# Rope and mixed key/value blocks from PSUM, gates copied raw, and the conv norm in another bank

## The chip, the core and the metric

The kernel runs on one core of a Trainium2 chip. The metric is the device time of one execution in microseconds. TensorE (PE) multiplies, VectorE (DVE), ScalarE (ACT) and GpSimd (POOL) do the rest on tiles of 128 partitions, and SyncE (SP) issues most DMAs. Each engine runs its own list of instructions in order; semaphores tie them together. Only TensorE, VectorE and ScalarE reach PSUM, which has 8 banks of 512 float32 per partition.

## The reference

Two blocks that share no data are computed in one program. The first is a hybrid state-space block (an SSD mixer and an S5 mixer, then an MLP). The second is a two-layer block on 512 latent tokens and 256 context tokens. The change is mostly in the second one's mixer. Cut to what matters:

```
p = h @ w_in                       # conv a|g, q, k, v, gates
q, k = rope_2d(q), rope_2d(k)
u = a * sigmoid(g); u = dwconv1d(u, 31 taps); u = silu(layernorm(u, ln_g, ln_b))
y_conv = u @ w_conv_out
y_attn = neighbourhood_attention(q, k, v, k_ctx, v_ctx, rpb) @ w_na_out
g_conv, g_attn = split(sigmoid(gates))
x = x + g1 * ((g_conv * y_conv + g_attn * y_attn) @ w_out)
```

Rope is `x * cos + rot(x) * sin`. Queries lie on a grid of 8 rows and 64 columns; each tile of 16 columns looks at a window of keys, and two of the six stored blocks of 128 keys are mixed from halves of two others.

## The kernel before

**Units.** All weights come as units of 128 output rows by 1024 inputs (512 KB). `U` counts them; unit g uses slot g % 4 (R = 4) of the weight buffers and of the PSUM accumulators. For a unit SyncE loads `wraw`, ScalarE copies it to `whi` (`split_hi`, line 257), GpSimd subtracts to `wlo` (`split_lo`, line 265), and TensorE makes three products for each of 8 input tiles (`pe_unit`, line 304, and `pe_quad` for four units together, line 338). `unit_done[s]` tells that a unit is finished, `acc_free[s]` that its accumulator has been read. A next load into a slot waits for the split or, where units are used whole (pass c0, `p.one`), for `unit_done`.

**Passes.** The second block has the passes c0 (context, layer 0, 256 columns, whole units), l0 (latent, layer 0, 512 columns), c1 (context of layer 1, keys and values only: `kv_pe`, `kv_act`, `kv_dve`) and l1. c0, l0 and l1 run `mix_*` and then `merge_*`, with units `p.U` to `p.U + 35` in the mixer: 8 for the conv branch, 12 for q, k, v of four head pairs, 16 gates. The merge has `M = p.U + 36` to `M + 7`.

**Attention.** 16 tiles in l0 and l1 (4 head pairs by 4 column tiles), 8 in c0. In each tile TensorE does the scores (`scores_pe`), transposes the probabilities of the tile before (`turn_pe`), makes the values of the one before that (`values_pe`), and one unit in between (`pe_filler`, lines 1945 to 1949; two in c0), whose result `pe_post` turns or transposes into bank 3. VectorE adds the bias and takes the maximum (`top_dve`), does a step of rope or of the values (`post_dve`), the reciprocal (`scale_dve`), and one or two rounds of conv taps (`conv_taps`, line 2240). ScalarE reads out the units (`evac_act`), exponentiates (`exps_act`, line 2106) and scales (`scale_act`). GpSimd does the conv taps of two more tiles and the `wlo` splits. The order is written out by hand in `mix_pe`, `mix_act`, `mix_dve` and `mix_pool`. `pe_post` of a step waits for the VectorE step before (`x_v`). The remaining conv taps of VectorE come after the last tile.

**Merge.** `merge_pe` multiplies the attention half of units M to M+3 (input tiles 4 to 7, banks 4 to 7), and in between the conv layernorm: a mean, a variance and a row of factors, all three in bank `p.U % R`, which is the bank of unit M's conv half. The conv halves of units M+1 to M+3 then go first, and unit M's follow. `merge_dve` multiplies by the gates `gt`.

**Other places.** `s5_pe` ends the S5 mixer with `ada_turn(7)`; ScalarE's `ada_cols(7)` and the last Gelu wait for it in order. `raw_pe` follows `ssd_pe`. `keep_busy(pe, bank, n)` is n products of 256 columns whose result nobody reads.

Of the kernel before, what the change touches and what calls it, by code (L numbers as in the profile page):

```python
# [120 lines left out]
def build(nc, A, out, ud, yd, pd):  # L121
# [1343 lines left out]
    def s5_pe(pe):  # L1465
# [8 lines left out]
        for i in range(NT):  # L1474
# [291 lines left out]
    rt = at("rt", [P, SEQ], O_HL + 12 * K)  # L1766
# [110 lines left out]
    def kv_act(act, p, then):  # L1877
# [3 lines left out]
        norm_root_act(act, n, then.T, "eps6")  # L1881
        for j in range(4):
            s, rnd = slot(p.U + j)
            act.wait_ge(unit_done[s], rnd + 2)
            act.activation(kctx[:, j], ps[:, s, 0:p.T], ACT.Copy).then_inc(acc_free[s], 1)
            split_hi(act, p.U + j + R)
# [183 lines left out]
    def evac_act(act, p, g):  # L2070
# [56 lines left out]
    def mix_act(act, p):  # L2127
# [40 lines left out]
        act.activation(lst[:, 0, 0:T // P], ps[:, p.U % R, 0:T // P], ACT.Sqrt, bias=col("eps6")).then_inc(p.c_a.sem, 1)  # L2168
# [9 lines left out]
    def post_dve(dve, p, i):  # L2178
# [3 lines left out]
        if k == 2:  # L2182
            v = ps[:, 3, 0:p.T].rearrange("p (b d) -> p b d", d=P)
            if p.lat:
                dve.tensor_copy(vT[:, 0:2], v[:, 0:2])
                dve.tensor_copy(vT[:, 4:6], v[:, 2:4])
                dve.drain()
                for m_, (lo, hi) in MIX.items():
                    dve.tensor_copy(vT[0:64, m_], vT[0:64, lo])
                    ins = dve.tensor_copy(vT[64:P, m_], vT[64:P, hi])  # L2190
            else:
                ins = dve.tensor_copy(vctx[:, :, h * P:(h + 1) * P], v)
        else:
# [49 lines left out]
    def mix_dve(dve, p):  # L2243
# [45 lines left out]
        for m in range(4):  # L2289
            dve.tensor_tensor(cn[:, m, 0:T], co[:, m, 0:T], ps[:, p.U % R, 0:T], ALU.subtract).then_inc(p.c_v.sem, 1)  # L2290
# [903 lines left out]
```

## Time and profile before

| | us |
|---|---|
| median of 3 runs | 2962.23 (2959.38 to 2964.63) |
| the profiled execution | 2951.68, span 2949.4 |
| TensorE busy | 2816.3 (95%) |
| VectorE busy | 1537.3 (52%) |
| GpSimd busy | 1274.6 (43%) |
| ScalarE busy | 1116.2 (38%) |
| mean granted TensorE clock | 0.981 of full |

Times in the trace count from the span's start. c0's mixer ends at about 1150 us and its merge at 1185. The attention of l0 runs from 1263 to 1456, its merge to 1546. c1 lies about 2143 to 2190, the attention of l1 from 2238 to 2430, its merge to 2520. Matmuls are pipelined and their ends are modelled, so a busy TensorE is not one at its peak; idle time in front of an instruction is named with what ended it. A granted clock of 1.00 is 2.4 GHz, of 0.50 1.2 GHz.

### The profile page before, as it was taken

The page shows a single profiled execution, that of the slowest core. Times are in us where ns is not written, and L with a number is a line of the kernel's source. Part 1 is how long each engine was busy: PE and PEld are TensorE (multiplying, and loading weights), DVE is VectorE, ACT ScalarE, POOL GpSimd, SP SyncE. Part 2 cuts the span into 40 slices and gives each one's busy share as a digit, 9 for nine tenths or more (in the row PEclk, how much of TensorE's full clock was granted, in tenths as well). Part 3 has the DMA queues.
Part 4 walks back from the last instruction along what each step waited for, and adds up shares of the span by engine and source line. Part 5 has one row for each costly group of instructions (what it writes and reads, how often), then busy time and mean ns, then how long its engine had stood idle before and what let it go on. Part 6 is the DMA issues. An engine that isn't in the chain of part 4 may idle for free.

```text
span 2949.4 us, 41217 instructions
## 1 busy us (share of the span) xinstructions
PE 2816.3 (95%) x15658; PEld 2297.0 (78%) x15658; DVE 1537.3 (52%) x1968; ACT 1116.2 (38%) x1666; POOL 1274.6 (43%) x696
## 2 busy tenths in 40 slices
PE   7999988999999999989999999999989999999998
PEld 6975734878888877867777888888877777788887
DVE  6865585353323255278775432423355867552525
ACT  4445223333323233236633422322343573342433
POOL 3444101435445173388842322222347784444443
PEclk9999998999999999999999999999999999999999
DMA  4235497323233233432222212122223222333332
GB/s 174 95 101 212 135 314 250 95 93 100 91 95 99 93 123 122 143 93 83 68 86 65 72 55 74 57 65 65 72 86 114 76 68 72 100 93 94 99 94 78
DMA packets 116008, 306.88 MB, mean 104 GB/s; under 512 B 36176, under 2 KB 44496, under 8 KB 115344
## 3 DMA queue, kind: packets, MB, share of 16 engines
q1 hardware_dynamic: 87584, 284.49, 30.5%
q10 hardware_dynamic: 27712, 18.50, 2.2%
q8 instruction: 100, 1.64, 0.2%
q0 software_dynamic: 560, 1.84, 0.2%
q14 instruction: 52, 0.43, 0.0%
HBM read 294.95 MB, written 7.45 MB: 103 GB/s over the span
## 4 chain that ended last, share of the span: by engine, by line
PE 77%; DVE 8%; DVEq 4%; ACT 3%; issue 2%; POOL 2%; DMA 2%; ACTq 1%; SPq 0%; POOLq 0%
PE ps L304 38%; PE ps L338 17%; PE ps L329 6%; PE ps L1941 3%; DVEq L2241 2%; POOL wlo L265 2%; DVE co L2240 2%; PE ps L2352 2%; PE ps L1945 1%; PE ps L1946 1%; PE ps L1949 1%; DMA mt<-ka 1%; PE ps L748 1%; DVE nacc L451 1%; PE ps L1999 1%
## 5 line engine op out<-in xcount | busy, mean ns | idle before, releaser
L265 POOL TENSOR_TENSOR wlo<-wraw,whi 128x1024 fp32r<-128x1024 f32 x373 | 923.1, 2484 | 1360.7 <-ACT whi L257 1359.3
L257 ACT ACTIVATE whi<-wraw 128x1024 fp32r<-128x1024 f32 x373 | 392.3, 1055 | 458.2 <-PE ps L304 170.5
L304 PE MATMUL ps<-xah,whi 128*128 128x512 f32 x992 | 387.9, 391 | 1.7 <-issue 1.7
L304 PE MATMUL ps<-xal,whi 128*128 128x512 f32 x992 | 387.4, 391 | 0.0
L304 PE MATMUL ps<-xah,wlo 128*128 128x512 f32 x992 | 280.1, 391 | 0.0
L2240 DVE SCALAR_TENSOR_TENSOR co<-ub,vec,co 128x512 f32<-128x512 f32 (+1 forms) x216 | 247.7, 1186 | 5.4 <-issue 0.4
L304 PEld LDWEIGHTS ps<-xah,whi 128*128 128x128 f32 x992 | 186.1, 188 | 42.8 <-issue 2.7
L304 PEld LDWEIGHTS ps<-xal,whi 128*128 128x128 f32 x992 | 186.1, 188 | 40.3
L304 PEld LDWEIGHTS ps<-xah,wlo 128*128 128x128 f32 x992 | 186.1, 188 | 40.2
L2339 POOL TENSOR_TENSOR co<-co,ct 128x512 f32<-128x512 f32 (+1 forms) x144 | 168.1, 1167 | 21.7 <-issue 1.8
L304 PE MATMUL ps<-hhi,whi 128*128 128x512 f32 x408 | 159.3, 390 | 1.1 <-ACT whi L257 1.1
L304 PE MATMUL ps<-hlo,whi 128*128 128x512 f32 x408 | 158.8, 389 | 0.0
L1109 DVE SCALAR_TENSOR_TENSOR res<-ps,mod,res 128x512 f32<-128x512 f32 (+1 forms) x64 | 47.7, 749 | 201.6 <-PE ps L329 110.0
L2687 DVE SCALAR_TENSOR_TENSOR f<-ps,vec,f 128x511 f32<-128x511 f32 x88 | 50.2, 612 | 196.6 <-ACT f L2648 196.6
L1945 PE MATMUL ps<-xah,whi 128*128 128x512 f32 x352 | 145.5, 413 | 4.2 <-DVE ub L2252 2.6
L2337 POOL TENSOR_TENSOR ct<-ub,vec 128x512 f32<-128x512 f32 (+1 forms) x144 | 136.5, 948 | 22.5 <-issue 12.4
L1946 PE MATMUL ps<-xal,whi 128*128 128x512 f32 x352 | 139.3, 396 | 0.0
L2645 ACT ACTIVATE f<-ps,vec 128x512 f32<-128x512 f32 x44 | 34.3, 780 | 186.9 <-PE ps L329 179.1
L1107 DVE TENSOR_TENSOR res<-res,ps 128x512 f32<-128x512 f32 x48 | 33.0, 688 | 132.2 <-PE ps L304 70.2
L304 PE MATMUL ps<-hhi,wlo 128*128 128x512 f32 x408 | 100.9, 389 | 0.0
L329 PE MATMUL ps<-xchi,whi 128*128 128x256 f32 x352 | 99.5, 283 | 0.0
L329 PE MATMUL ps<-xchi,wlo 128*128 128x256 f32 x352 | 99.3, 282 | 0.0
(419 smaller groups left out, 6065.1 us busy)
## 6 DMA issues: line engine op xcount, KB each, us to landing
wraw<-stream SPq DMA_DIRECT2D x425, 512.0 KB, 3.5
wada<-w_ada SPq DMA_DIRECT2D x56, 512.0 KB, 7.4
wraw<-w_ada SPq DMA_DIRECT2D x40, 512.0 KB, 3.9
biasb<-attn_bias ACTq DMA_DIRECT2D x32, 256.0 KB, 3.6
xin<-x0T SPq DMA_DIRECT2D x4, 528.0 KB, 6.7
s_u<-uk ACTq DMA_DIRECT2D x8, 264.0 KB, 2.5
res<-x0T ACTq DMA_DIRECT2D x1, 2048.0 KB, 9.5
outT<-res SPq DMA_DIRECT2D x4, 512.0 KB, 2.6
```

What stands on the lines that cost most here:

```text
L257: act.activation(whi[:, s], wraw[:, s], ACT.Copy).then_inc(hi_done[s], 1)
L265: pool.tensor_tensor(wlo[:, s], wraw[:, s], whi[:, s].bitcast(F32), ALU.subtract).then_inc(lo_done[s], 1)
L304: last = pe.matmul(ps[:, bank, 0:b - a], w[:, s, kt], x[:, kt, c0 + a:c0 + b], start=start, stop=stop)
L329: return pe.matmul(ps[:, R + s, 0:CTX], w[:, s, kt], part[:, kt], start=start, stop=stop)
L338: last = pe.matmul(ps[:, bank, 0:b - a], w[:, s, kt], x[:, kt, c0 + a:c0 + b], start=start, stop=stop)
L1941: last = pe.matmul(o, wraw[:, s, kt], x1[:, kt, 0:p.T], start=kt == 0, stop=kt == NT - 1)
L1945: pe.matmul(o, whi[:, s, kt], xah[:, kt, 0:p.T], start=kt == 0, stop=False)
L1946: pe.matmul(o, whi[:, s, kt], xal[:, kt, 0:p.T], start=False, stop=False)
L2240: dve.scalar_tensor_tensor(o, ub[:, m, k:k + p.T], colr(f"dw{p.l}", 1, k * 4 + m), o, ALU.mult, ALU.add)
L2241: dve.drain()
L2337: pool.tensor_tensor(ct[:, 0:T], ub[:, m, k:k + T], colr(f"dw{l}", 1, k * 4 + m).to_broadcast([P, T]), ALU.mult)
L2339: ins = pool.tensor_tensor(o, o, ct[:, 0:T], ALU.add)
```

## The change

1. `s5_pe`: `keep_busy(pe, 1, 8)` ahead of the last `ada_turn`.
2. After `ssd_pe`: `keep_busy(pe, 5, 4)`.
3. `kv_act`: the root of the norm comes after the first `kctx` copy and no longer ahead of it.
4. `evac_act`: gates of units below `p.U + 30` are copied raw from PSUM; in `mix_act` two Sigmoids in place follow each of the units `p.U + 29` to `p.U + 33`.
5. `post_dve`: the product with the sine is written back into PSUM bank 3, and each add reads it there. The two mixed key blocks are made by four adds of 64 columns in place of four copies; the mixed value blocks are copied from PSUM and not from the stored blocks. A drain goes in each.
6. Conv norm: mean, variance and row use the bank of unit M+3. The mean waits until the last gate has left that bank. The conv halves run over units M to M+2 first, and unit M+3 comes last.

```diff
             if i in ADA_END:
                 pe.wait_ge(f_a.sem, f_a.past("bat", min(i + 2, NT - 1)))
+                if i == NT - 1:
+                    keep_busy(pe, 1, 8)
                 ada_turn(pe, ADA_END[i])
...
-        norm_root_act(act, n, then.T, "eps6")
         for j in range(4):
             s, rnd = slot(p.U + j)
             act.wait_ge(unit_done[s], rnd + 2)
             act.activation(kctx[:, j], ps[:, s, 0:p.T], ACT.Copy).then_inc(acc_free[s], 1)
+            if j == 0:
+                norm_root_act(act, n, then.T, "eps6")
             split_hi(act, p.U + j + R)
...
-            act.activation(gt[:, h, 0:p.T], a, ACT.Sigmoid).then_inc(acc_free[s], 1)
+            act.activation(gt[:, h, 0:p.T], a, ACT.Sigmoid if g >= p.U + 30 else ACT.Copy).then_inc(acc_free[s], 1)
...
         for g in range(p.U + 29, p.U + 36):
             evac_act(act, p, g)
+            d = 2 * (g - p.U - 29)
+            for h in range(d, min(d + 2, 30 - GATE0)):
+                act.activation(gt[:, h, 0:T], gt[:, h, 0:T], ACT.Sigmoid)
...
-                dve.drain()
                 for m_, (lo, hi) in MIX.items():
-                    dve.tensor_copy(vT[0:64, m_], vT[0:64, lo])
-                    ins = dve.tensor_copy(vT[64:P, m_], vT[64:P, hi])
+                    dve.tensor_copy(vT[0:64, m_], v[0:64, lo - 2])
+                    ins = dve.tensor_copy(vT[64:P, m_], v[64:P, hi])
...
-            dve.tensor_tensor(rt[:, :], ps[:, 3, :], sinT, ALU.mult)
+            t = ps[:, 3, :]
+            dve.tensor_tensor(t, t, sinT, ALU.mult)
             dve.drain()
             if k == 0:
-                ins = dve.tensor_tensor(bycol(qT[:, :]), grid(x), grid(rt[:, :]), ALU.add)
+                ins = dve.tensor_tensor(bycol(qT[:, :]), grid(x), grid(t), ALU.add)
             else:
+                def keys(at, c, n):
+                    o = kT[:, at:at + GH * n].rearrange("p (c r) -> p c r", r=GH)
+                    return dve.tensor_tensor(o, grid(x)[:, c:c + n], grid(t)[:, c:c + n], ALU.add)
+
                 for a in range(2):
-                    o = kT[:, 4 * P * a:4 * P * a + 2 * P].rearrange("p (c r) -> p c r", r=GH)
-                    c = slice(32 * a, 32 * a + 32)
-                    dve.tensor_tensor(o, grid(x)[:, c], grid(rt[:, :])[:, c], ALU.add)
-                dve.drain()
+                    keys(4 * P * a, 32 * a, 32)
                 for m_, (lo, hi) in MIX.items():
-                    dve.tensor_copy(kT[:, m_ * P:m_ * P + 64], kT[:, lo * P:lo * P + 64])
-                    ins = dve.tensor_copy(kT[:, m_ * P + 64:m_ * P + P], kT[:, hi * P + 64:hi * P + P])
+                    keys(m_ * P, 16 * (lo - 2), 8)
+                    ins = keys(m_ * P + 64, 16 * hi + 8, 8)
...
     def conv_mean_pe(pe, p):
         pe.wait_ge(p.c_v.sem, p.c_v.past("acc"))
-        pe.matmul(ps[:, p.U % R, 0:p.T], ones512, lmu[:, 0:p.T], start=True, stop=True).then_inc(p.c_p.sem, 1)
+        pe.matmul(ps[:, (p.U + 3) % R, 0:p.T], ones512, lmu[:, 0:p.T], start=True, stop=True).then_inc(p.c_p.sem, 1)
...
-        pe.wait_ge(acc_free[M % R], read_out(M - R))
+        pe.wait_ge(acc_free[(M + 3) % R], read_out(M - 1))
...
         all_freed(pe, M)
-        for kt in range(4):
+        for kt in range(2):
             pe.wait_ge(p.c_h.sem, p.c_h.past("hi", kt))
-            for j in range(1, R):
-                last = hi_part(j, kt)
...
+            for j in range(R - 1):
+                hi_part(j, kt)
             if kt and not p.one:
+                pe.wait_ge(p.c_lo.sem, p.c_lo.past("lo", 0))
+                for j in range(R - 1):
+                    lo_part(j, 0)
+        if p.one:
+            pe.wait_ge(p.c_h.sem, p.c_h.past("hi", 3))
+            for j in range(R):
+                for kt in range(2 if j < R - 1 else 0, 4):
+                    last = hi_part(j, kt)
+                counted(j, last)
...
-            for kt in range(4):
-                last = lo_part(0, kt)
-            counted(0, last)
-            for j in range(1, R):
-                counted(j, lo_part(j, 3))
+            for j in range(R - 1):
+                counted(j, lo_part(j, 3))
+            for kt in range(4):
+                last = lo_part(R - 1, kt)
+            counted(R - 1, last)
...
             ssd_pe(pe)
+            keep_busy(pe, 5, 4)
             raw_pe(pe, U_OUT1, "ssd", hhi, hlo, lambda: raw_sums_ssd(pe), lambda: s5_first_pe(pe))
```

## Rows read from the trace of the kernel before

**Rows 1.** TensorE's waits by releaser: us in total, times, longest.
```profile
PE ps L1962 <- DVE kT L2208: 9.9, 5, 2.9
...
PE ps L1987 <- ACT pex L2106: 5.5, 5, 2.0
...
PE ps L2309 <- DVE lmu L2286: 3.8, 2, 3.3
PE ps L1999 <- ACT pex L2114: 3.4, 7, 0.9
```

**Rows 2.** Six stretches: span, busy PE, PEld, DVE, ACT, POOL, clock, DMA, GB/s.
```profile
319.80:330.00 10.20, 10.20 (x38) 9.04 (x38) 0.18 (x1) 0.27 (x1) 0.00 (x0) 0.50 0.17 27
507.50:514.30 6.80, 6.15 (x14) 4.55 (x15) 2.17 (x11) 0.63 (x1) 2.92 (x2) 0.50 0.76 223
1169.70:1173.10 3.40, 3.17 (x8) 2.54 (x9) 3.16 (x8) 1.26 (x2) 0.00 (x0) 0.51 1.01 412
1292.60:1296.00 3.40, 3.40 (x10) 2.62 (x9) 3.02 (x6) 0.57 (x1) 3.12 (x4) 0.50 0.32 128
2265.40:2272.20 6.80, 6.24 (x20) 4.44 (x21) 3.37 (x8) 0.49 (x1) 6.21 (x6) 0.50 0.26 80
2412.20:2415.60 3.40, 3.40 (x16) 2.33 (x14) 3.33 (x4) 3.37 (x5) 0.99 (x1) 0.50 0.01 2
```

**Rows 3.** VectorE in l0's attention by shape: busy, mean ns; last: line 2208, ns min/median/max.
```profile
L2204 DVE TENSOR_TENSOR kT<-raw,rt 128x256 f32<-128x256 f32 x8 | 9.4, 1218 | 0.3
L2195 DVE TENSOR_TENSOR raw<-raw,cst 128x512 f32<-128x512 f32 x8 | 9.0, 1125 | 4.8 <-PE ps L1964 4.8
L2189 DVE COPY vT<-vT 64x128 f32<-64x128 f32 x8 | 5.9, 742 | 0.3
L2196 DVE TENSOR_TENSOR rt<-ps,cst 128x512 f32<-128x512 f32 x8 | 5.4, 680 | 0.0
L2190 DVE COPY vT<-vT 64x128 f32<-64x128 f32 x8 | 4.7, 582 | 0.1
...
L2207 DVE COPY kT<-kT 128x64 f32<-128x64 f32 x8 | 4.5, 565 | 0.3
...
L2185 DVE COPY vT<-ps 128x256 f32<-128x256 f32 x4 | 1.7, 415 | 0.0
...
L2208 DVE COPY kT<-kT x16: 181/182/2383, 1288.3 to 2352.7; 128x64 f32<-128x64 f32 x16
```

**Rows 4.** ScalarE groups (busy, mean ns); then VectorE in time, idle before.
```profile
L257 ACT ACTIVATE whi<-wraw 128x1024 fp32r<-128x1024 f32 x27 | 28.3, 1050 | 0.0
...
L2078 ACT ACT_TABLE_LOAD x8 | 10.3, 1283 | 0.1
L2078 ACT ACTIVATE gt<-ps 128x512 f32<-128x512 f32 x14 | 8.4, 598 | 25.1 <-PE ps L304 16.7 <-PE ps L1949 8.3
...
1395.32 0.17 DVE L2226 RECIPROCAL sm<-sm 128x2 f32<-128x2 f32 x1 [3.38 <-ACT pex L2106]
1395.40 4.50 DVE L2240 SCALAR_TENSOR_TENSOR co<-ub,vec,co 128x512 f32<-128x512 f32 x4
...
1413.66 0.17 DVE L2226 RECIPROCAL sm<-sm 128x2 f32<-128x2 f32 x1 [1.52 <-ACT pex L2106]
```

**Rows 5.** Merges: c0's conv halves in the chain; TensorE behind c0's and l0's.
```profile
1159.12 7.16 PE ps L2352 x32
...
1169.93 0.80 PE L304 MATMUL ps<-h,wraw 128*128 128x256 f32 x1 [3.67 <-DMA wraw<-stream]
...
1524.52 0.50 PE L304 MATMUL ps<-hhi,whi 128*128 128x512 f32 x1 [0.53 <-ACT whi L257]
```

**Rows 6.** GpSimd in c1, in order of time: six splits in a row.
```profile
2175.98 15.03 POOL L265 TENSOR_TENSOR wlo<-wraw,whi 128x1024 fp32r<-128x1024 f32 x6 [13.31 <-ACT whi L257]
```

**Rows 7.** TensorE in order of time, where it begins again after the two places.
```profile
307.79 0.50 PE L338 MATMUL ps<-hhi,whi 128*128 128x512 f32 x1 [1.94 <-ACT hhi L488]
...
508.15 0.79 PE L338 MATMUL ps<-hhi,wlo 128*128 128x512 f32 x1 [2.25 <-POOL wlo L265]
```

More of the change, by code:

```diff
@@ L2167, in mix_act @@
         act.wait_ge(p.c_p.sem, p.c_p.past("var"))
-        act.activation(lst[:, 0, 0:T // P], ps[:, p.U % R, 0:T // P], ACT.Sqrt, bias=col("eps6")).then_inc(p.c_a.sem, 1)
+        act.activation(lst[:, 0, 0:T // P], ps[:, (p.U + 3) % R, 0:T // P], ACT.Sqrt, bias=col("eps6")).then_inc(p.c_a.sem, 1)
         for m in range(4):
@@ L2289, in mix_dve @@
         for m in range(4):
-            dve.tensor_tensor(cn[:, m, 0:T], co[:, m, 0:T], ps[:, p.U % R, 0:T], ALU.subtract).then_inc(p.c_v.sem, 1)
+            dve.tensor_tensor(cn[:, m, 0:T], co[:, m, 0:T], ps[:, (p.U + 3) % R, 0:T], ALU.subtract).then_inc(p.c_v.sem, 1)
         dve.wait_ge(p.c_a.sem, p.c_a.past("sq1"))
@@ L2301, in mix_dve @@
         for m in range(4):
[L2302 removed]
+            dve.scalar_tensor_tensor(lsq[:, m, 0:T], cn[:, m, 0:T], colr(f"lng{l}", 1, m), ps[:, (p.U + 3) % R, 0:T], ALU.mult, ALU.mult).then_inc(p.c_n.sem, 1)
         for m in range(0 if p.one else 4):
@@ L2313, in conv_var_pe @@
         for j in range(p.T // P):
-            last = pe.matmul(ps[:, p.U % R, j:j + 1], lmu[:, j * P:(j + 1) * P], ones512[:, 0:1], start=True, stop=True)
+            last = pe.matmul(ps[:, (p.U + 3) % R, j:j + 1], lmu[:, j * P:(j + 1) * P], ones512[:, 0:1], start=True, stop=True)
         last.then_inc(p.c_p.sem, 1)
@@ L2319, in conv_row_pe @@
         for j in range(p.T // P):
-            last = pe.matmul(ps[:, p.U % R, j * P:(j + 1) * P], lst[:, 1, j:j + 1].to_broadcast([P, P]), ident, start=True, stop=True)
+            last = pe.matmul(ps[:, (p.U + 3) % R, j * P:(j + 1) * P], lst[:, 1, j:j + 1].to_broadcast([P, P]), ident, start=True, stop=True)
         last.then_inc(p.c_p.sem, 1)
@@ L2397, in merge_pe @@
         all_freed(pe, M)
-        for kt in range(4):
+        for kt in range(2):
             pe.wait_ge(p.c_h.sem, p.c_h.past("hi", kt))
-            for j in range(1, R):
-                last = hi_part(j, kt)
-                if p.one and kt == 3:
-                    counted(j, last)
-            if kt == 2:
-                pe.wait_ge(p.c_n.sem, p.c_n.past("n", 3))
-                hi_part(0, 0)
-                hi_part(0, 1)
-            if kt >= 2:
-                last = hi_part(0, kt)
-                if p.one and kt == 3:
-                    counted(0, last)
-            if kt and not p.one:
+            for j in range(R - 1):
+                hi_part(j, kt)
+            if kt and not p.one:
+                pe.wait_ge(p.c_lo.sem, p.c_lo.past("lo", 0))
[7 more added lines that the diff above has]
+                counted(j, last)
+        else:
+            for kt in range(2, 4):
+                pe.wait_ge(p.c_h.sem, p.c_h.past("hi", kt))
+                for j in range(R - 1):
+                    hi_part(j, kt)
+                if kt == 2:
+                    pe.wait_ge(p.c_n.sem, p.c_n.past("n", 3))
+                    hi_part(R - 1, 0)
+                    hi_part(R - 1, 1)
+                hi_part(R - 1, kt)
                 pe.wait_ge(p.c_lo.sem, p.c_lo.past("lo", kt - 1))
-                for j in range(1, R):
+                for j in range(R - 1):
                     lo_part(j, kt - 1)
-        if not p.one:
             pe.wait_ge(p.c_lo.sem, p.c_lo.past("lo", 3))
+            for j in range(R - 1):
+                counted(j, lo_part(j, 3))
             for kt in range(4):
-                last = lo_part(0, kt)
-            counted(0, last)
-            for j in range(1, R):
-                counted(j, lo_part(j, 3))
+                last = lo_part(R - 1, kt)
+            counted(R - 1, last)
         def summed(m):
```

2 lines of the change are left out of this document (removed).

## The prediction

> **What bounds the kernel now.** I read the chain of waits first. It lies mostly on TensorE, so an edit elsewhere is worth only the TensorE idle time that it ends, plus the clock that such an idle time costs later. The second view is therefore the list of what TensorE waited for [rows 1]. In the attention of the passes l0 and l1 it waited 9.9 us, in 5 places, for the keys that VectorE writes (`post_dve`, `L2208`). It waited 5.5 us and 3.4 us for the exponentials and scaled probabilities of ScalarE (`L2106`, `L2114`), and 3.8 us for the conv branch sum (`L2286`). The third view is the granted clock by stretch [rows 2]: each of six stretches of 3.4 to 10.2 us shows 0.5, the 1.2 GHz level. Before five of them TensorE had idled for 2.0 us or more, the five waits that the parts below name; before the sixth, at 319.8 us, it had run one-column products, with no idle.
>
> **Rope and mixed blocks from PSUM.** This touches only the passes with `lat`, l0 and l1, 4 heads each. Now a k post is one product with both inputs in SBUF, one with an input in PSUM, two adds of 256 columns and four copies of 64; a v post is two PSUM copies and four SBUF copies. The group rows of l0 [rows 3] tell the reader why the order of operands matters. The product with a PSUM input takes 0.68 us, the same-sized one with two SBUF inputs 1.13 on average, beside a busy GpSimd. The copies `L2207` and `L2208` move 64 columns; `L2207` averages 0.57 us, and `L2208` goes from 0.18 to 2.38.
> Per k post now: 1.13 + 0.68 + 2 x 1.22 + 4 x 0.57 = 6.5 us. After: 1.13 + 0.68, two adds of 256 columns with one PSUM input, and four adds of 64. No row has an add with strided PSUM input. Bounds: 0.41 us for 256 columns (the contiguous PSUM copy `L2185`), and 1.22 (`L2204`). I take 0.7, between them and nearer the PSUM row, and 0.25 for 64 columns: 1.8 + 1.4 + 1.0 = 4.2 us. The saving is 2.3 us, between 0 and 3.
> Per v post the four SBUF copies cost 2 x 0.74 + 2 x 0.58 = 2.6 us. From PSUM, at half of 0.41 and up to 0.41 each, they cost 0.8 to 1.6. I take 1.2: 1.4 us saved, and one drain fewer. The q add loses an SBUF operand: 0 to 0.5 us.
> The 9.9 us of waits are five, the longest 2.9. That one comes where an `L2208` copy took 2.38 us; the new form has no such copy, so its saving there is nearer 4 us. I keep 0.9 and count **9.0 us**. The half-clock stretches at 1292.6 and 2265.4 stand right behind the longest key wait of each pass; TensorE was busy 3.40 and 6.24 us in them [rows 2], and at the full 2.4 GHz the same work takes half. That is 1.7 + 3.1 = **4.8 us**.
> The Trainium skill (SBUF — State Buffer, "Who interferes with whom") says that VectorE and GpSimd share one port pair as an exclusive lock, and that VectorE with at most one SBUF input does not contend; the steady 0.68 us beside the uneven 1.13 agrees. A rule of the skill speaks against the edit: VectorE: DVE Perf Modes, "Why PSUM operands drop a tier", says an fp32 copy from PSUM loses the doubled rate. By it alone the new v copies would be slower, not faster.
>
> **Gates copied raw.** Ten gates of each pass leave PSUM as Copy, and ten Sigmoids follow in place behind gates `U+29` to `U+33`. The table loads around them go. In l0 these are 8 loads of 1.28 us for gates [rows 4] and as many for exponentials; after the change one of each is left. Most are hidden. They end the chain only where the maximum was ready first: there VectorE waited 3.38 us from maximum to exponentials, where a tile whose load was early shows 1.52 [rows 4]; the difference, 1.86, is the load, 1.28, and a DMA issue ahead of it. Such exposed tiles come twice in l0 and twice in l1. The 5.5 + 3.4 us of waits come after them, because lateness is handed from tile to tile: VectorE's taps take 4.5 us in one tile and more in others, so its cycle and TensorE's are close. Taking 1.28 from two tiles and some 1.4 from the last v post makes VectorE 4 us less late per pass. I count 5.9 of 8.9 us as gone, and keep 3.0 for taps that still collide. The bounds are 2.6 and 8.9. The stretch at 2412.2 follows the longest such wait, 2.0 us [rows 1, 2]: 3.40 / 2 = 1.7. Together **7.6 us**. In c0 TensorE had no such wait: nothing. The ten Sigmoids are in the cover of the last gate units: ScalarE has an evacuation of 0.60 and a split of 1.05 us per unit [rows 4] and now 2 x 0.6 more, one load once, 2.9 to 4.1 us against 24 products of 0.22 = 5.4 us (the rate is 7.16 / 32 [rows 5]). Without the cover they would cost 7 us per pass.
> The Trainium skill (ScalarE: Activation LUTs, "What ACT_TABLE_LOAD costs") puts a switch at about 2.66 us, with a drain. The row after the load does not show that drain, and the sum uses 1.28. By the page four exposures would give 5.5 us more.
>
> **Conv norm in the fourth bank.** In c0 the merge stage has 32 products in 7.16 us, then 3.67 us idle for a weight DMA [rows 5]. That DMA needs unit M done, and unit M was among the last. In the new order unit 0 has its last product after 8 of 16 pairs, 3.6 us earlier, and the idle time falls to about 0.2: 3.5 us. The half-clock stretch behind it, 3.17 / 2 = 1.6 [rows 2], goes too. In l0 and l1 the next unit waited 0.53 us for the split of slot 0 [rows 5]; unit M is now counted 6 products before the end, not 3, or 0.7 us earlier: 2 x 0.53. The added wait, the freed bank of the last gate, is met: the conv sum comes later still. Behind it would stand all of the merge. Sum **6.2 us**, between 3.5 and 6.3.
>
> **Root after the first copy, in `kv_act`.** The root waits for a sum issued after the whole quad, while unit 0 is done earlier. GpSimd then runs six splits in a row, 15.03 us or 2.5 each [rows 6], and TensorE waits for the last of the chain. The first split moves ahead of the sum, so the chain is one split shorter: **2.4 us**, between 0 (a weight DMA or the norm ends last instead) and 3.5.
>
> **The two fillers.** Each `keep_busy` product passes in two records of 0.22 us. Four make 1.8 us, in an idle time of 1.94 [rows 7]: 0, between -1.5 (half clock) and +0.3. The stretch at 319.8 [rows 2] comes 12 us later, and stays. In the S5 stage eight make 3.6 us ahead of the last turn. TensorE then waits 2.25 us [rows 7] for a split of GpSimd that hangs on neither, so the 3.6 us lie mostly in cover; the Gelu on ScalarE is about 1 us later, with its result wanted much later. What can be won is the half clock at 507.5 [rows 2], 6.15 / 2 = 3.1 us. Some idle time remains there, so I take half: **1.5 us**, between -2 and 3.1.
>
> **Sum.** 9.0 + 4.8 + 7.6 + 6.2 + 2.4 + 0 + 1.5 = 31.5 us. The profiled execution took 2951.7 us (span 2949.4), 10.5 below the median of 2962.2; both move alike: 2962.2 - 31.5 = **2930.7 us**. What is late next is the conv tail of VectorE, 26 taps after the last tile in both l passes. It starts from TensorE's unit `U+28`, so it moves along with the gain; its own collisions can take 3.8 us off or put 3.3 on.
>
> **Rivals.** (A) *The taps rule.* In the gate tiles VectorE and GpSimd, not the loads, set the cycle. For it: GpSimd has a 2.5 us split and four tap operations per tile. Against it: the 3.38 beside 1.52. Then gates give 2.6 of 7.6, the fillers 0 and the tail costs 3: 2962.2 - 31.5 + 5.0 + 1.5 + 3 = 2940. Chance 0.20. (B) *The copies are not the limiter.* Colliding first products keep half of the key waits and their clock: 13.8 / 2 = 6.9 less, with A's losses: 2947; 0.08. (C) *The skill's price of a table switch*: 5.5 us more where exposed; the waits to be ended then cap it at 3.0, so 2927.7; 0.04. (D) *The change gives nothing measurable*, as conv tails and splits take the time back: 2960; 0.05. (E) *Slower: strided PSUM reads.* Each k post reads 768 strided PSUM columns and each q post 512. At 10 ns a column, not the 2.7 assumed, a head costs 9.3 us more on VectorE; about 2.5 of that is slack, so 8 heads cost 55 us, against 17.7 us that the other parts keep: 3000. It decides from about 5.5 ns a column. Against it: the PSUM product is steady at 0.68. Chance 0.05. The forecast has 0.58.
>
> The range is 2918 to 2952: all waits gone with the tail lucky (14.7 + 10.6 + 6.3 + 3.5 + 3.1 + 3.8 = 42), and only the surer parts with the tail unlucky (7 + 2.6 + 3.5 - 3 = 10). A difference under 0.2%, 6 us, can't be told from none. Faster 0.89 (forecast, A, B, C), same 0.06, slower 0.05.
>
> **What would show it.** Right: no TensorE wait for `kT` over 0.5 us; four steady adds of 64 columns near 0.25 us; one load per pass in the gate tiles; under 0.5 us idle before the first unit behind c0's merge; full clock behind both key posts; root 3 us after the first `kctx` copy. Wrong: adds with PSUM input over 1.2 us, ScalarE waits replaced by waits for `wlo`, or a conv tail over 42 us.

## The result, and the profile after

The changed kernel takes 2922.84 us (median of 4 runs, 2919.9 to 2925.17) against 2960.81 of the kernel before beside it (4 runs, 2956.88 to 2964.63). The ratio is 0.9871, 95% interval 0.9854 to 0.9888: 33 to 43 us less. Forecast were 31.5 us less and 2930.7; the 31.5 lie just below this interval. In the two profiled executions the difference is 28.1 us (2951.68 to 2923.63), which is below it too; the first experiment is about this.

TensorE's waits, by what ended them (us in total, times, longest), answer to [rows 1]:

```profile
PE ps L2001 <- ACT pex L2116: 6.9, 8, 1.9
...
PE ps L1989 <- ACT pex L2108: 2.4, 4, 0.8
...
PE ps L1966 <- DVE qT L2204: 0.4, 2, 0.2
```

No wait for `kT` and none for the conv sum `lmu` is left; together they were 13.7 us. The waits for exponentials and probabilities were 5.5 + 3.4 = 8.9 us and are 6.9 + 2.4 = **9.3 us**: these the change did not end.

The granted clock in seven stretches (span, busy PE, PEld, DVE, ACT, POOL, clock, DMA, GB/s). The first six lie where [rows 2] lie, shifted; the last is new:

```profile
321.00:331.20 10.20, 10.20 (x37) 8.68 (x37) 0.18 (x1) 0.27 (x1) 0.00 (x0) 0.63 0.26 42
509.50:512.90 3.40, 3.23 (x9) 2.03 (x8) 0.00 (x0) 0.08 (x1) 1.86 (x1) 0.50 0.68 206
1164.90:1168.30 3.40, 3.37 (x16) 2.98 (x17) 3.16 (x8) 1.26 (x2) 0.00 (x0) 1.00 0.96 361
1282.00:1285.40 3.40, 3.40 (x19) 2.56 (x16) 2.72 (x5) 0.82 (x2) 2.96 (x4) 1.00 0.48 137
2243.00:2249.80 6.80, 6.80 (x36) 5.32 (x35) 3.10 (x7) 2.13 (x3) 6.36 (x5) 1.00 0.26 78
2383.00:2386.40 3.40, 2.88 (x30) 2.27 (x32) 3.26 (x5) 2.79 (x5) 1.56 (x2) 1.00 0.01 2
1430.90:1434.30 3.40, 3.40 (x24) 2.77 (x24) 3.33 (x4) 1.26 (x2) 2.06 (x1) 0.53 0.00 0
```

Four of the six run at the full 2.4 GHz now. The 0.63 of the first row is no gain: its half-clock stretch lies at 318.4 to 328.6 us and is 10.2 us long, as before, and the window shown reaches past its end. The last row begins behind a wait of 1.94 us for probabilities, at the last gate tile of l0: in place of one half-clock stretch in l1 there is one in l0.

VectorE in l0's attention by shape (busy, mean ns), as [rows 3]:

```profile
L2199 DVE TENSOR_TENSOR raw<-raw,cst 128x512 f32<-128x512 f32 x8 | 8.3, 1038 | 4.9 <-PE ps L1966 4.9
L2201 DVE TENSOR_TENSOR ps<-ps,cst 128x512 f32<-128x512 f32 x8 | 5.5, 686 | 0.0
L2208 DVE TENSOR_TENSOR kT<-raw,ps 128x256 f32<-128x256 f32 x8 | 4.6, 619 | 0.7 <-issue 0.4
L2204 DVE TENSOR_TENSOR qT<-raw,ps 128x512 f32<-128x512 f32 x4 | 4.4, 1099 | 0.3
...
L2208 DVE TENSOR_TENSOR kT<-raw,ps 128x64 f32<-128x64 f32 x16 | 3.1, 256 | 0.0
...
L2194 DVE COPY vT<-ps 64x128 f32<-64x128 f32 x8 | 2.4, 295 | 0.1
L2193 DVE COPY vT<-ps 64x128 f32<-64x128 f32 x8 | 2.2, 278 | 0.1
```

A k post is now 1.04 + 0.69 + 2 x 0.62 + 4 x 0.26 = 4.0 us; forecast were 4.2. The adds of 64 columns are steady: all 32 of l0 and l1 lie between 0.251 and 0.267 us, where the copies `L2208` went from 0.18 to 2.38. The add for the queries reads its 512 columns with a stride and takes 1.10 us, the product with the sine reads as many in a row and takes 0.69.

VectorE in order of time over l0's last gate tiles (start, us, ..., idle before), as the end of [rows 4]:

```profile
1388.41 7.01 DVE L2246 SCALAR_TENSOR_TENSOR co<-ub,vec,co 128x512 f32<-128x512 f32 x4
...
1399.16 6.02 DVE L2246 SCALAR_TENSOR_TENSOR co<-ub,vec,co 128x512 f32<-128x512 f32 x4
...
1429.20 0.17 DVE L2232 RECIPROCAL sm<-sm 128x2 f32<-128x2 f32 x1 [1.51 <-ACT pex L2108]
1429.28 5.97 DVE L2246 SCALAR_TENSOR_TENSOR co<-ub,vec,co 128x512 f32<-128x512 f32 x4
...
```

ScalarE's table loads in the same attention, all of them:

```profile
L2108 ACT ACT_TABLE_LOAD x1 | 1.3, 1283 | 2.6 <-DVE sm L2227 2.6
```

The loads are gone, and the last four tiles show the short 1.51 or 1.52 us from maximum to reciprocal. But their four taps take 5.0 to 6.0 us, and 7.0 in the tile before. The 4.5 of [rows 4] was one tile: in the trace of before the four taps take 2.9 to 7.7 us in the six gate tiles of l0, and the mean over l0 and l1 is 5.3 us. After the change that mean is 6.0.

The chain of waits behind c0's merge, as [rows 5]:

```profile
1157.58 3.71 PE ps L2358 x16
...
1161.46 3.42 DMA wraw<-stream
```

TensorE where it goes on:

```profile
1164.93 1.35 PE L304 MATMUL ps<-h,wraw 128*128 128x256 f32 x5 [0.21 <-DMA wraw<-stream]
```

And GpSimd in c1, as [rows 6]:

```profile
2157.57 15.05 POOL L265 TENSOR_TENSOR wlo<-wraw,whi 128x1024 fp32r<-128x1024 f32 x6 [13.01 <-ACT whi L257]
```

The weight DMA starts with 3.71 us of products behind c0's last wait, not with 7.16, and TensorE waits 0.21 us for it, not 3.67. GpSimd's six splits of c1 are as they were.

### The profile page after: what moved, and what is told of

It is laid out like the page before. It is cut to its first block, busy times and chain, and to the rows that moved or that the text cites. A ratio compares the mean times of both kernels' runs of the same rounds, so it can differ in the third digit from the quotient of the medians.

```text
span 2921.7 us, 41245 instructions
## 1 busy us (share of the span) xinstructions
PE 2814.4 (96%) x15682; PEld 2298.1 (79%) x15682; DVE 1511.5 (52%) x1968; ACT 1084.6 (37%) x1662; POOL 1263.9 (43%) x696
## 4 chain that ended last, share of the span: by engine, by line
PE 82%; DVE 5%; ACT 3%; DVEq 2%; POOL 2%; issue 2%; DMA 2%; ACTq 1%; SPq 0%; POOLq 0%
PE ps L304 40%; PE ps L338 17%; PE ps L329 6%; PE ps L1943 3%; POOL wlo L265 2%; PE ps L1947 2%; PE ps L2358 2%; PE ps L1948 2%; PE ps L1951 2%; DVEq L2247 1%; DMA mt<-ka 1%; PE ps L2020 1%; PE ps L2001 1%; PE ps L748 1%; DVE co L2246 1%
## 5 line engine op out<-in xcount | busy, mean ns | idle before, releaser
L304 PE MATMUL ps<-xah,whi 128*128 128x512 f32 x992 | 387.9, 391 | 1.7 <-issue 1.7
L304 PE MATMUL ps<-xal,whi 128*128 128x512 f32 x992 | 387.4, 391 | 0.0
L304 PE MATMUL ps<-xah,wlo 128*128 128x512 f32 x992 | 280.1, 391 | 0.0
L2246 DVE SCALAR_TENSOR_TENSOR co<-ub,vec,co 128x512 f32<-128x512 f32 (+1 forms) x216 | 255.8, 1223 | 5.1
L304 PEld LDWEIGHTS ps<-xah,whi 128*128 128x128 f32 x992 | 186.1, 188 | 42.7 <-issue 2.7
L304 PEld LDWEIGHTS ps<-xal,whi 128*128 128x128 f32 x992 | 186.1, 188 | 40.3
L304 PEld LDWEIGHTS ps<-xah,wlo 128*128 128x128 f32 x992 | 186.1, 188 | 40.1
L2345 POOL TENSOR_TENSOR co<-co,ct 128x512 f32<-128x512 f32 (+1 forms) x144 | 159.4, 1107 | 21.7 <-issue 1.8
L304 PE MATMUL ps<-hhi,whi 128*128 128x512 f32 x408 | 159.2, 390 | 0.0
L304 PE MATMUL ps<-hlo,whi 128*128 128x512 f32 x408 | 158.8, 389 | 0.0
L1109 DVE SCALAR_TENSOR_TENSOR res<-ps,mod,res 128x512 f32<-128x512 f32 (+1 forms) x64 | 47.6, 748 | 201.7 <-PE ps L329 110.0
L2343 POOL TENSOR_TENSOR ct<-ub,vec 128x512 f32<-128x512 f32 (+1 forms) x144 | 134.5, 934 | 22.5 <-issue 12.4
L304 PE MATMUL ps<-hhi,wlo 128*128 128x512 f32 x408 | 100.9, 389 | 0.0
```

The costliest lines, as they stand in the source:

```text
L304: last = pe.matmul(ps[:, bank, 0:b - a], w[:, s, kt], x[:, kt, c0 + a:c0 + b], start=start, stop=stop)
L2246: dve.scalar_tensor_tensor(o, ub[:, m, k:k + p.T], colr(f"dw{p.l}", 1, k * 4 + m), o, ALU.mult, ALU.add)
L2343: pool.tensor_tensor(ct[:, 0:T], ub[:, m, k:k + T], colr(f"dw{l}", 1, k * 4 + m).to_broadcast([P, T]), ALU.mult)
L2345: ins = pool.tensor_tensor(o, o, ct[:, 0:T], ALU.add)
```

## Where the time went, stretch by stretch

I cut TensorE's timeline of every run at the same instructions. (1) c0's merge: from the first conv half (`L2352` in before) to the next norm's row (`L532`). (2) Attention: from the first product of the mixer (`L1945`) to the first unit behind the last tile (`L304`), l0 and l1 added. (3) From there to the mean of the conv norm (`L2309`). (4) From the mean to the first unit behind the conv halves. (5) All else behind the start of the S5 mixer's merge units. In us:

| kernel | (1) | (2) | (3) | (4) | (5) | sum |
|---|---|---|---|---|---|---|
| before | 52.4 | 396.1 | 73.3 | 51.8 | 1836.3 | 2409.9 |
| before, again | 52.8 | 393.4 | 75.7 | 53.6 | 1835.0 | 2410.4 |
| rope from PSUM alone | 52.4 | 381.7 | 72.9 | 52.0 | 1836.4 | 2395.5 |
| gates raw alone | 54.0 | 394.0 | 69.2 | 50.3 | 1834.3 | 2401.7 |
| fourth bank alone | 47.5 | 396.0 | 73.2 | 50.5 | 1835.8 | 2402.9 |
| after, gates at once | 47.6 | 385.1 | 72.2 | 48.9 | 1834.8 | 2388.7 |
| after | 47.3 | 381.5 | 69.2 | 48.9 | 1835.1 | 2382.0 |
| after, again | 47.5 | 381.5 | 69.2 | 48.9 | 1834.6 | 2381.6 |

The stretches ahead of (5) end between 527 and 536 us, and differ also where two kernels are alike up to there. The two traces of before show how far a row can be trusted: the sums agree within 0.5 us, single stretches differ by up to 2.7.

## The experiments

Times are medians; the ratio is to the kernel before, run beside it, with its 95% interval.

**Before, again.** No edit.

> The kernel before, unchanged, to see how far two profiled executions of one program lie apart. The two medians differ by 38.0 us, the two profiled executions by 28.1. Theory P: the profiled execution of before (2951.7, 9 us under its median) was a lucky one, with fewer half-clock stretches or shorter collisions of GpSimd and VectorE than usual; then this run's median is 2960 +- 3, its trace has a span of some 2956 or more, and the extra time lies in a place that can be named. Rival Q: the 10 us are the chip on which it ran; then the ratio is 1.000 and the trace here agrees with the first one stage by stage within 1 us.

2958.95 us (2949.83 to 2963.54) against 2956.3; ratio 1.0003 (0.9991 to 1.0016). The profiled execution took 2949.83, the shortest of its twelve. So P is right that the profiled executions of before were on the short side, but its sign, a span of some 2956 here, did not come: the span is 2948.0. Q's ratio came, and the sums behind the S5 mixer agree within 0.5 us, though not each stretch within 1; but the twelve executions were on one chip and lie between 2949.8 and 2963.5, so another chip is not needed to explain the 10 us. Ahead of the merge of S5 the traces differ by up to 8 us. The time of an execution goes with its granted clock: of the 85 timed executions of before in these experiments, the 13 with a mean clock of 0.983 or more average 2949.6 us and the 11 with 0.979 or less 2961.4. What makes one execution get more half-clock time than the next stays open. The two traces show that it need not follow from the waits: in the attention of l0 and l1 TensorE has 13.6 us at half clock in the first and 3.4 in this one, with 22.5 and 23.7 us of idle time. The stretches behind the S5 mixer are the sharper measure, and I use them below.

**Rope and mixed blocks alone.** Part 5 of the diff, on the kernel before.

> Before with part 5 alone (rope and mixed key and value blocks from PSUM). By the steps of the prediction this part is worth 9.0 us of waits and 4.8 us of clock: 13.8 us, 2947. No TensorE wait for the keys over 0.5 us, where there were 9.9 us in 5 places; the key adds at 0.62 and 0.26 us as after the whole change; the half-clock stretches behind the key posts of both passes gone. If the conv tail's shortening (3.3 us of wait for the sum, and the clock behind it, in l0) also comes from VectorE being earlier, then it shows here too and the part is worth 18 to 20 us. Rival: the gain shows only together with the gates; then the waits for the exponentials grow by what the key waits lose, and under 8 us is left.

2938.91 us, 0.994 (0.9921 to 0.9958): 12 to 23 us. By the table 14.7 us less than the mean of the two traces of before, 13.0 of it in the attention. No wait for `kT`. The conv tails hardly took part (36.7 and 37.2 us, where before has 36.7 to 37.5), so by the stretches the gain is near the 13.8 of the forecast and not 18 to 20 (the medians, 17.4 us apart, can't tell). The rival is out: the waits for `pex` are 6.3 + 2.0 = 8.3 us, and were 8.9.

**Gates alone.** Part 4 of the diff, on the kernel before.

> Before with part 4 alone (gates copied raw, Sigmoids late). The prediction's forecast: 5.9 us of the 8.9 us of waits for exponentials and probabilities go, and 1.7 us of clock: 7.6 us. Rival A (VectorE's taps set the cycle of the gate tiles, not the table loads): 2.6 us or less. The trace after the whole change shows 9.3 us of such waits, not fewer, with no load of a table left in those tiles and taps at 6 to 7 us for four; so now I hold A: the waits stay between 7 and 10 us, and the gain is 0 to 3 us.

2948.35 us, 0.9977 (0.9962 to 0.9992). Each of the two had one half right. The waits are as A says:

```profile
PE ps L1999 <- ACT pex L2114: 7.0, 8, 2.0
```

with 2.3 us more ahead of the scores, 9.3 together. Yet the trace is 8.4 us shorter, near the forecast of 7.6. The attention has only 0.7 of it; stretch (3) has 5.3 and (4) 2.4: the gain is in the conv tail and what hangs on it.

**After, gates at once.**

```diff
-            act.activation(gt[:, h, 0:p.T], a, ACT.Sigmoid if g >= p.U + 30 else ACT.Copy).then_inc(acc_free[s], 1)
+            act.activation(gt[:, h, 0:p.T], a, ACT.Sigmoid).then_inc(acc_free[s], 1)
```

> The changed kernel with part 4 undone: Sigmoid at once from PSUM, no late Sigmoids. If the loads matter once the keys are early, the waits for exponentials and probabilities grow from 9.3 to 13 us or more and the time by 5 us or more over the changed kernel's 2922.8. If VectorE's cycle of taps, bias, maximum and reciprocal (9.8 us a tile, of which 6.0 for four taps) is what sets the gate tiles, an early load is partly hidden and the time grows by 0 to 4 us. If the raw gates are a loss (ten more ScalarE operations), it falls.

2934.08 us, 0.9929 (0.9906 to 0.9951), 11 over the changed kernel's first median, 6.9 by the table (mean of the two traces of after). The waits are 6.2 + 5.4 = 11.6 us. 3.6 us of the loss are attention, 3.0 are stretch (3). That is between what I had named: the loads matter some (11.6 us of waits in place of 9.3), but the 13 us of the first case did not come.

**After, again.** No edit.

> The changed kernel, unchanged, beside the next three on one chip: the median 2923 +- 3. It also tests where executions of one program differ. Counting the trace from the start of the S5 merge on (TensorE's first product of the units behind the last turn's quad), before has 2409.9 and 2410.4 us in its two traces and the changed kernel 2382.0, while the stretch ahead of that differs by up to 8 us between kernels that are the same there. If that is so, this trace has 2382.0 +- 1 behind that point, and both conv tails of 33.2 us.

2924.2 us against 2955.39, 0.9897 (0.9878 to 0.9915); 2381.6 us in the table, tails 33.21 and 33.20 us. As expected. The two comparisons of the change give 38.0 and 31.2 us by medians, and 28.3 by the stretches.

**One tap ahead of the reciprocal.**

```diff
             if n in post_at:
                 post_dve(dve, p, post_at[n])
+            if p.lat and n >= 10:
+                ks = list(itertools.islice(taps, 2))
+                conv_taps(dve, p, ks[:1], (2,))
             scale_dve(dve, p, n)
...
-            if n < p.N:
-                some(1 if p.lat and n < 10 else 2)
+            if p.lat and 10 <= n < p.N:
+                conv_taps(dve, p, ks[:1], (3,))
+                conv_taps(dve, p, ks[1:])
+            elif n < p.N:
+                some(1 if p.lat else 2)
```

> The changed kernel, and in the gate tiles of l0 and l1 (tiles 10 to 15) one of the four conv taps stands between maximum and reciprocal, where VectorE idles 1.52 us for the exponentials; the other three stay behind the reciprocal. Theory (VectorE's cycle sets these tiles: 0.76 + 1.23 + 1.52 + 0.17 + 6.0 + 0.16 = 9.8 us against TensorE's 9.0): the cycle falls by up to 1.3 us, below TensorE's, the 9.3 us of waits for exponentials and probabilities fall to 3 or less, and 5 to 8 us are gained. Rival 1: a split of GpSimd holds that tap for 2.9 us, so that the reciprocal is 1.4 us late and the wait is as long as before: 0 +- 2. Rival 2: the conv tail meets GpSimd in a worse phase (its last tap over 8 us after the tail's start) and is 37 us again, 3 us back per pass.

**2914.01 us**, 0.986 (0.984 to 0.988): the fastest kernel here, 10 under the changed one beside it. The attention takes 369.4 us in place of 381.5, and no wait for `pex` is left; by the stretches it is 13.5 us faster, more than the 5 to 8 expected. VectorE in one gate tile:

```profile
1414.91 1.22 DVE L2227 TENSOR_REDUCE sm<-ps 128x2 f32<-128x1024 f32 x1
1416.05 0.74 DVE L2246 SCALAR_TENSOR_TENSOR co<-ub,vec,co 128x512 f32<-128x512 f32 x1
1417.65 0.17 DVE L2232 RECIPROCAL sm<-sm 128x2 f32<-128x2 f32 x1 [0.85 <-ACT pex L2108]
1417.73 3.89 DVE L2246 SCALAR_TENSOR_TENSOR co<-ub,vec,co 128x512 f32<-128x512 f32 x3
```

In this tile the tap of 0.74 us fits into the idle time, and the reciprocal is not later. In the last gate tile of l0 it meets a split and takes 1.97 us, and the reciprocal is 0.8 us later; rival 1 is true of that tile. The four taps also take less, 4.6 us here and 5.3 in the mean of l0's gate tiles, not 6.0. So VectorE's cycle with its taps did set these tiles. The tail is 36.0 us (rival 2, in part), but it starts earlier and TensorE doesn't wait for it.

**Root behind the first split.**

```diff
-            if j == 0:
-                norm_root_act(act, n, then.T, "eps6")
             split_hi(act, p.U + j + R)
+            if j == 0:
+                norm_root_act(act, n, then.T, "eps6")
```

> The changed kernel with the root of kv_act behind the first split and not ahead of it. The prediction counted 2.4 us for part 3 as if the first split moved ahead of the root; in the code only the first copy does, and the trace after shows the chain of six GpSimd splits still starting behind the root. Theory: the first GpSimd split starts 3 us earlier (some 4.5 us behind the last product of the quad, before the root), the chain of six ends 2.4 us earlier, and TensorE's waits after it (1.30, 1.24 and 1.11 us) fall by 1 to 2.4 us in sum. Rival: the weight DMA (1.03 us in the trace after) or the norm of l1 ends last instead: under 0.5 us.

2928.75 us against 2924.2 of the changed kernel beside it, whose ratios overlap (0.9905, 0.9883 to 0.9926). GpSimd in order of time in c1:

```profile
2161.38 2.38 POOL L265 TENSOR_TENSOR wlo<-wraw,whi 128x1024 fp32r<-128x1024 f32 x1 [9.71 <-ACT whi L257]
2164.78 18.74 POOL L265 TENSOR_TENSOR wlo<-wraw,whi 128x1024 fp32r<-128x1024 f32 x7 [1.02 <-ACT whi L257]
```

TensorE's waits behind it:

```profile
2180.79 0.50 PE L338 MATMUL ps<-xah,wlo 128*128 128x512 f32 x1 [2.01 <-POOL wlo L265]
...
2183.57 0.80 PE L338 MATMUL ps<-xah,wlo 128*128 128x512 f32 x1 [1.20 <-POOL wlo L265]
```

The first split does come earlier and the waits of 1.30 and 1.24 us are gone, but the chain is seven splits long now and its end makes TensorE wait 3.2 us in one place, where it was 1.1. In sum 0.4 us of wait is won. Behind the bunched waits the granted clock is 0.50 for 6.8 us, from 2181.95 on, where the changed kernel has 1.00; in return its half-clock stretch of 3.4 us at 2158.1 is not there. In sum nothing is won: from the norm's sums in c1 (`L524`) to l1's mixer TensorE takes 65.1 us, and 64.5 and 64.4 in the two traces of the changed kernel.

**No fillers.** Both `keep_busy` calls taken out of the changed kernel.

> The changed kernel without its two fillers. Forecast of the prediction: 1.5 us slower (the S5 filler won 1.5, the other 0). The traces: the S5 filler takes 3.7 us and ends 1.5 us of short waits, the wait for a GpSimd split is 2.0 in place of 2.25, and a half-clock stretch of 6.8 us has become one of 3.4. By that it is a loss of 0.6 us, so without it -0.6 to +1; the median can't tell, the trace can: the span from the last keys of the S5 mixer to the 16th product of the merge.

2928.99 us, 0.9906 (0.9887 to 0.9925), not to be told from the changed kernel. From the end of the S5 keys to the first merge unit TensorE takes 29.4 us here; over all traces it is 28.7 to 31.0 in seven without the S5 filler (mean 29.6) and 29.2 to 31.6 in seven with it (30.2). The S5 filler is worth nothing that can be seen.

**Fourth bank alone.** Part 6 of the diff, on the kernel before.

> Before with part 6 alone (conv norm in the fourth bank, unit M+3 last). The prediction's terms: 5.1 us in c0 (3.5 of wait for a weight DMA, 1.6 of clock) and 0.53 in each of l0 and l1, 6.2 us together. The traces with the whole change show the stretch from the first conv half of c0 to the next norm's row at 47.3 to 47.6 us against 52.4 to 54.0 in the kernels without this part, and the stretch of the latent merges at 24.45 against 25.1 to 26.8. So: -5 us in c0, -0.7 in each latent merge, nothing elsewhere, 2949 by the median. Rival: the added wait for the fourth bank or the sum shows as an idle TensorE ahead of the mean: 1 us or more lost there.

2948.4 us, 0.9988 (0.9977 to 0.9999). The trace has 7.2 us less: 5.1 in c0's merge, 2.2 in the latent merges against the mean of both traces of before, 1.3 against the nearer one. No wait ahead of the mean that was not there: the rival is out.

**Product with the sine in SBUF.**

```diff
-            t = ps[:, 3, :]
-            dve.tensor_tensor(t, t, sinT, ALU.mult)
+            t = rt[:, :]
+            dve.tensor_tensor(t, ps[:, 3, :], sinT, ALU.mult)
```

> The changed kernel, but the product with the sine is written to the SBUF tile rt again, so that the adds for queries, keys and mixed key blocks have both inputs in SBUF; the mixed blocks are still made by four adds of 64 columns and the value blocks still come from PSUM. It tells apart what frees the key post: the operand in PSUM or the copies left out. If GpSimd's hold on the SBUF port is the cause, the adds of 256 columns take 1.2 us again (0.62 now) and some of those of 64 columns 1 to 2.5 us (0.26 now), TensorE waits for kT 3 to 8 us in sum, and 4 to 12 us are lost. If it is enough that the copies and the drain between are gone, the waits stay under 1 us and the time within 2 us of the changed kernel.

2947.9 us, 0.9978 (0.9966 to 0.9989): 24 us over the changed kernel, from the place of one operand. By the stretches 20.0 us, 21.2 in the attention. VectorE by shape in l0's attention:

```profile
L2209 DVE TENSOR_TENSOR kT<-raw,rt 128x64 f32<-128x64 f32 x16 | 11.6, 794 | 0.0
...
L2209 DVE TENSOR_TENSOR kT<-raw,rt 128x256 f32<-128x256 f32 x8 | 9.5, 1230 | 0.7 <-issue 0.4
```

TensorE's wait for the keys:

```profile
PE ps L1965 <- DVE kT L2209: 13.6, 6, 4.0
```

The same adds take 0.79 in place of 0.26 us and 1.23 in place of 0.62, and the wait is longer than the 9.9 us of before. I had expected 3 to 8 us of waits and a loss of 4 to 12: the direction is as expected, the size nearly twice that. So making the mixed blocks by adds is no gain with both inputs in SBUF; the gain lies in that they read PSUM.

**One tap ahead of the reciprocal, gates at once.** The edits of the fourth and the sixth run together.

> The kernel with the tap ahead of the reciprocal, but part 4 undone: Sigmoid at once, so two table loads in each gate tile. With that tap in the cover of the exponentials VectorE's cycle is some 8.5 us, TensorE's 9.0; a load of 1.28 us that is exposed makes 9.8 again. If loads matter once the taps do not, TensorE's waits for exponentials and probabilities go from 0 to 4 to 8 us, GpSimd is later at the conv tail (its last tap over 8 us behind the tail's start), and 5 to 10 us are lost over that kernel's 2914. If they lie in cover, the waits stay under 2 us and the loss under 3.

2920.87 us, 0.9892 (0.9877 to 0.9906), 7 over the kernel with the tap alone; by the stretches 10.0. The waits for `pex` are 0.7 + 0.6 us: the loads lie in cover, and my 4 to 8 us were wrong, as was the loss of under 3 us that I had tied to this case. The loss is in the tail, where I had named it too: 6.2 us in stretch (3), 1.6 in (4). GpSimd where the tail of l0 begins:

```profile
1437.33 1.29 POOL L2348 TENSOR_TENSOR co<-co,ct 128x512 f32<-128x512 f32 x1
1438.59 2.85 POOL L265 TENSOR_TENSOR wlo<-wraw,whi 128x1024 fp32r<-128x1024 f32 x1
```

VectorE's tail:

```profile
1438.44 37.15 DVE L2243 SCALAR_TENSOR_TENSOR co<-ub,vec,co 128x512 f32<-128x512 f32 x26
```

Its first tap meets a whole split, and TensorE waits 5.9 us in the two passes for the sum.

**GpSimd's last round of taps left out.** On the kernel before.

```diff
-POOL_TAPS = 22
+POOL_TAPS = 21
...
-        conv_taps(dve, p, range(p.taps, KTAP), (0, 1))
+        conv_taps(dve, p, range(p.taps if p.one else 22, KTAP), (0, 1))
```

> Before, but GpSimd's last round of conv taps (two products and two adds, about 6 us) is left out in l0 and l1; VectorE's 26 taps of the tail are all still made, so the output lacks one tap of two of the four conv tiles. It tests what sets the length of the conv tail. Fourteen tails in the traces so far: 33.2 to 33.7 us where GpSimd's last tap ends 6.7 us after the tail's start, 36.7 to 37.5 where it ends 7.9 to 9.3 after it. Theory: GpSimd's taps, and the extra split that they push into the tail, hold VectorE (a tap is 0.75 us alone and 2.9 under a split); without that round both tails are 33 to 34.5 us though VectorE's work is the same, and TensorE's wait for the sum in l0 goes from 3.3 to under 1 us: 4 to 8 us faster in all. Rival: the tail is long for VectorE's own count or for ScalarE's later evacuations; then it stays at 36.7 to 37.5 us and the time within 2 us of before.

(The 36.0 us tails with the tap ahead of the reciprocal, where GpSimd's last tap ends at 7.2 us, belong between the two groups of that sentence.) 2946.2 us, 0.9972 (0.9961 to 0.9983). VectorE's 26 taps of the tail, in l0 and l1:

```profile
1460.16 20.04 DVE L2240 SCALAR_TENSOR_TENSOR co<-ub,vec,co 128x512 f32<-128x512 f32 x16
1480.62 11.64 DVE L2240 SCALAR_TENSOR_TENSOR co<-ub,vec,co 128x512 f32<-128x512 f32 x10 [0.43 <-issue]
...
2431.41 31.68 DVE L2240 SCALAR_TENSOR_TENSOR co<-ub,vec,co 128x512 f32<-128x512 f32 x26
```

32.1 and 31.7 us, against 37.5 and 36.7 for the same taps and shorter than the 33 to 34.5 expected, and no wait for the sum. By the stretches 8.1 us are won. The theory holds: GpSimd's work beside it sets the length of the tail. VectorE also waits by semaphore for GpSimd's last tap, after 8 of its 26; that is not it, as VectorE idles 0.15 us at most in that place in every trace.

## Why the prediction was right, and where it was not

**Rope: right in mechanism and in sum, not in its two terms.** 13.8 us forecast; 14.7 alone, by the stretches. The adds cost 0.62 and 0.26 us (forecast 0.7 and 0.25), a v post's four copies 2 x 0.28 + 2 x 0.30 = 1.15 (forecast 1.2), the q add lost 0.06. The doubtful step, from steady PSUM rows to a steady PSUM add, is what the run with the product in SBUF shows: the same add is 2 to 3 times as long with its second input in SBUF. Rivals B, D and E are out. E had a point that the forecast passed over: reading with a stride costs something, 1.10 us against 0.69 for 512 columns. But that is 2.1 ns a column, 2.4 for 256 and 4 for 64, where E put 10 and needed 5.5 (its own terms give 6.4 for a change that gains nothing). The rule of the Trainium skill (SBUF — State Buffer, "Who interferes with whom") that VectorE and GpSimd exclude one another on a shared port pair agrees with this. So does another rule of the Trainium skill (VectorE: DVE Perf Modes, "Why PSUM operands drop a tier") for a copy alone on the port: line 2190's SBUF copy has a minimum of 0.22 us, the PSUM copy takes 0.28. It is the mean, 0.58 to 0.74 with GpSimd beside it, that decided here.

How the 13.8 us divide was wrong, and that the sum came out is luck. The idle time of TensorE in the attention, l0 and l1 added, is 22.5 and 23.7 us in the two traces of before and 11.9 with this part alone: 11.2 us less, where 9.0 were counted. The half-clock time there is 13.6 and 3.4 us in the same two traces, and 6.8 with this part. Half of the difference is what the clock gives back: 0.9 us against the mean of the two, between 3.4 more and 1.7 less against either, where 4.8 were counted from one trace.

**Gates: the size right, the steps wrong.** 7.6 us forecast, 8.4 alone, 6.9 on top of the others. But the step "taking 1.28 from two tiles makes VectorE 4 us less late", and with it 5.9 us of ended waits, failed: 8.9 us became 9.3. I had the cycles "close" and took the load for the later of the two. Rival A's mechanism was the true one: with the loads gone, the four taps beside GpSimd take 5.0 to 7.0 us, VectorE's cycle is 9.8 us in most of these tiles, TensorE's is 8.8 where it has no wait (in the run with the tap ahead), and moving one tap ends the waits that removing the loads did not. Rival A's price was wrong too: it had the tail cost 3 us more, and the tail is where the gates pay. Its 33.2 to 33.7 us, in both passes and in every kernel with raw gates and the old taps, against 36.7 to 37.5 in most others, I had named only as collisions that can take 3.8 off or put 3.3 on. So the forecast of this part was met by luck. Rival C is out: the load is 1.28 us, the next activation starts at once, and with the tap ahead of the reciprocal two loads per tile are hidden.

**Bank: right.** 6.2 us forecast; 5.1 in c0 and 1.3 to 2.2 in the latent merges.

**Root: a misreading.** The prediction has "the first split moves ahead of the sum"; the diff moves only the 0.38 us copy, and the split still stands behind the root. From c1's norm to l1's mixer 0.3 us are won, not 2.4. The run with the root behind the split shows that the edit I had read into it would not have brought 2.4 either.

**S5 filler: nothing, not 1.5.** It bought some half-clock time with 3.7 us of its own, of which only 1.5 us of short waits was cover. The half-clock stretch behind the first of those units is 3.4 or 6.8 us in the seven traces without it (mean 4.4) and 0 or 3.4 in the seven with it (mean 1.5); half of the difference is 1.5 us. **Other filler: 0, as forecast**: the wait of 1.94 us is gone, filled.

**The sum.** 31.5 forecast; rope 0.9 more, gates 0.7 less, bank 0.2 more (5.1 + 1.3), root 2.1 less, filler 1.5 less: 28.3, which is what the stretches show. The medians have 31 and 38. That the forecast lies so near rests partly on the tail, which paid for the waits that stayed. The lower end of the range, 2918, is 2 us under its own sum (2962.2 - 42 = 2920.2); nothing hangs on it.

**The signs named ahead.** No wait for `kT`; 64-column adds at 0.26; one load for the exponentials in l0's attention; 0.21 us idle behind c0's merge; full clock behind both key posts; the root 3.3 us behind the first copy: all came. None of them would have shown that the gates' waits stay. I should have named the waits for `pex` under 3.0 us among them.

## What to carry to other kernels

Where VectorE and GpSimd run side by side, put one operand of VectorE's short operations in PSUM if it has been there anyway: it makes them short and, more, steady. An idle time that recurs in a cycle (here maximum to reciprocal) is worth an operation moved into it before anything is removed elsewhere. Price a tail of queued operations by what runs beside it when it starts, and read a moved line in the diff for what stands between its old and its new place. Don't price half-clock time from one trace: in the attention of the same kernel it was 13.6 us in one execution and 3.4 in another.

## What the runs showed of the hardware

A conv tap of VectorE (512 columns, two inputs in SBUF) takes 0.75 us alone, and one that begins under a split of GpSimd ends 0.54 to 0.56 us behind that split, however early or late in it the tap began (327 taps in the 14 traces, with over 1 us of the split still to come). Beside a tap operation of GpSimd it takes 1.52 us at the median and 1.85 at most. VectorE in l0's tail of the changed kernel, one tap under a split and one alone:

```profile
1450.95 2.88 DVE L2246 SCALAR_TENSOR_TENSOR co<-ub,vec,co 128x512 f32<-128x512 f32 x1
...
1454.57 0.75 DVE L2246 SCALAR_TENSOR_TENSOR co<-ub,vec,co 128x512 f32<-128x512 f32 x1
```

GpSimd beside it:

```profile
1450.64 2.65 POOL L265 TENSOR_TENSOR wlo<-wraw,whi 128x1024 fp32r<-128x1024 f32 x1 [0.16 <-issue]
1455.06 2.52 POOL L265 TENSOR_TENSOR wlo<-wraw,whi 128x1024 fp32r<-128x1024 f32 x1 [1.77 <-ACT whi L257]
```

GpSimd pays much less: its split is 2.4 us alone and at most 2.9 beside taps. So a split that falls into VectorE's tail costs it some 2.1 us: with a round less, six splits fall into a tail that is 12.4 us longer than 26 taps alone. In all other traces seven do. How long the tail is then goes with how much of GpSimd's taps and of the split ahead of them it meets: in l0 of before it begins under a split and its first tap takes 2.52 us, in l0 of the changed kernel behind it, and 0.99. In order of where GpSimd's last tap ends:

| GpSimd's last tap ends behind the tail's start | tail, 26 taps |
|---|---|
| 0.4 us ahead of it, 0.1 us behind it (a round less) | 32.1, 31.7 us |
| 6.7 us (raw gates; l0 with gates at once) | 33.2 to 33.7 us |
| 7.2 us (tap ahead of the reciprocal) | 36.0 us |
| 7.9 to 9.3 us (the others) | 36.7 to 37.5 us |
